# A rotary kernel whose swapped halves are copied out of PSUM by ScalarE instead of moved by DMA

## The reference

```python
def rope(x, positions):
    half = x.shape[-1] // 2
    ...
    x1, x2 = xf[..., :half], xf[..., half:]
    out = jnp.concatenate([x1 * cos - x2 * sin, x2 * cos + x1 * sin], axis=-1)

qa = rope(...); ka = rope(...)          # 24 heads each
qd = rope(...); kd = rope(...)          # 8 x 2 halves each
```

## Time and profile before

| | |
|---|---|
| median of 3 runs | 877.96 us (875.67 to 879.02) |
| the profiled execution, own time | 879.07 us |
| its span, first to last instruction | 877.3 us |
| TensorE busy | 818.3 us, 93% |
| VectorE, ScalarE, GpSimd busy | 471.5, 359.8, 482.6 us (54, 41, 55%) |
| mean granted TensorE clock | 0.982 of full |

### The profile page before, as it was taken

One profiled execution on the slowest core, in us unless ns is written; L12 is line 12 of the kernel. 1 busy time (PEld: TensorE's weight loads), 2 busy tenths in 40 slices (PEclk: granted clock), 3 DMA queues, 4 the chain that ended last, 5 costly groups with the idle time before them and its releaser, 6 DMA issues.

```text
span 877.3 us, 12629 instructions
## 1 busy us (share of the span) xinstructions
PE 818.3 (93%) x4622; PEld 687.9 (78%) x4622; DVE 471.5 (54%) x751; ACT 359.8 (41%) x774; POOL 482.6 (55%) x625
## 2 busy tenths in 40 slices
PE   1579799999999999999998999999899999999997
PEld 0468589788888888888877878778777777888897
DVE  2785678454454536323568669759756644102622
ACT  3334444344444344432444454454546542223410
POOL 2564655345655647245858359759645637736300
PEclk9979899999999999999998999999999999999999
DMA  9774284222333233324353133333121213333521
GB/s 251 198 217 105 67 285 121 86 73 86 96 121 94 80 117 97 97 72 137 105 138 96 49 110 97 109 97 86 57 88 49 60 37 117 99 97 106 182 97 49
DMA packets 92852, 94.87 MB, mean 108 GB/s; under 512 B 8269, under 2 KB 84086, under 8 KB 92662
## 3 DMA queue, kind: packets, MB, share of 16 engines
q1 hardware_dynamic: 92496, 93.64, 35.4%
q0 software_dynamic: 240, 0.39, 0.5%
q10 hardware_dynamic: 54, 0.02, 0.0%
HBM read 78.21 MB, written 5.34 MB: 95 GB/s over the span
## 4 chain that ended last, share of the span: by engine, by line
PE 69%; DVE 13%; issue 6%; DMA 4%; ACT 4%; SPq 2%; POOL 2%; DVEq 0%; POOLq 0%; ACTq 0%
PE proj L1502 50%; PE score L1381 4%; PE proj L1580 4%; PE sums L1427 3%; PE turned L1398 3%; DMA ada<-in_w_ada 2%; DVE dstat L1145 2%; PE score L1356 2%; ACT probs L891 2%; PE sums L1429 2%; DVE ada_sum L1025 1%; DVE dstat L1161 1%; DVE q_lo L1106 1%; DVE at_lo L1168 1%; ACT junk L923 1%
## 5 line engine op out<-in xcount | busy, mean ns | idle before, releaser
L694 POOL TENSOR_TENSOR w_lo<-raw,w_hi 128x256 fp32r<-128x256 f32 x392 | 316.4, 838 | 224.4 <-ACT w_hi L807 224.4
L1502 PE MATMUL proj<-h_hi,w_hi 128*128 128x512 f32 x608 | 253.3, 417 | 6.8 <-POOL h_lo L704 5.7
L1502 PE MATMUL proj<-h_hi,w_lo 128*128 128x512 f32 x608 | 241.8, 398 | 0.0
L1502 PE MATMUL proj<-h_lo,w_hi 128*128 128x512 f32 x608 | 241.0, 396 | 0.0
L1502 PEld LDWEIGHTS proj<-h_hi,w_hi 128*128 128x128 f32 x608 | 116.3, 191 | 42.1 <-issue 8.6
L1502 PEld LDWEIGHTS proj<-h_hi,w_lo 128*128 128x128 f32 x608 | 116.5, 192 | 26.6
L1502 PEld LDWEIGHTS proj<-h_lo,w_hi 128*128 128x128 f32 x608 | 116.7, 192 | 21.1
L807 ACT ACTIVATE w_hi<-raw 128x1024 fp32r<-128x1024 f32 x100 | 104.2, 1053 | 12.0 <-PE proj L1502 7.8
L719 POOL TENSOR_TENSOR rope_x<-rope_x,cos_t 128x512 f32<-128x512 f32 x36 | 55.9, 1552 | 69.5 <-DMA rope_s<-rope_x 69.5
L1168 DVE TENSOR_TENSOR at_lo<-turned,at_hi 128x512 fp32r<-128x512 f32 x64 | 43.9, 687 | 60.3 <-ACT at_hi L909 59.7
L891 ACT ACTIVATE probs<-score,dstat 128x512 f32<-128x512 f32 x64 | 43.4, 684 | 59.9 <-DVE dstat L1145 59.9
(11 more groups left out here) (245 smaller groups left out, 1522.1 us busy)
## 6 DMA issues: line engine op xcount, KB each, us to landing
raw<-in_w_in SPq DMA_DIRECT2D x88, 512.0 KB, 3.6
rope_s<-rope_x SPq DMA_DIRECT2D x144, 64.0 KB, 2.4
ada<-in_w_ada SPq DMA_DIRECT2D x16, 512.0 KB, 6.3
zd<-in_w_ada SPq DMA_DIRECT2D x8, 512.0 KB, 5.2
raw<-in_w_proj_b SPq DMA_DIRECT2D x8, 512.0 KB, 3.4
raw<-in_w_out SPq DMA_DIRECT2D x8, 512.0 KB, 4.1
rows_in<-window_rows SPq DMA_DIRECT2D x4, 792.0 KB, 4.9
window_rows<-rows_out SPq DMA_DIRECT2D x4, 528.0 KB, 4.9
```

Of the source, the lines that this page charges most:

```text
L694: ins = nc.gpsimd.tensor_tensor(lo[:, k, :], raw[:, n % RAW, k, :], hi.bitcast(F32)[:, k, :], ALU.subtract)
L1502: ins = mm(dst, left, right, start=k == 0 and n == 0, stop=k == nk - 1 and n == 2)
```

## The change

`rope_copy` gets four more ScalarE instructions. After the copy of the whole bank it copies the bank again, one quarter of the partitions at a time, each into the place of its neighbour in `rope_s` (or in the upper half of `zd`), with the same scale. The four DMAs of a tile, the four larger ones of the first four tiles, and their waits on SyncE go. GpSimd's cosine product now waits for the first copy only, VectorE's sine product for the last quarter, and TensorE's reuse of the bank for the last quarter too.

```diff
-        def swapped_wait(engine, tile):
-            n = rope_no[tile.u]
-            if n < 4:
-                engine.wait_ge(first_swapped, 64)
-            else:
-                engine.wait_ge(swapped[n % 4], 64 * (n // 4))
...
-            def swap_heads(tile):
-
-                n = rope_no[tile.u]
-                sp.wait_ge(rope_copied, n + 1)
-                if n >= 6:
-                    sp.wait_ge(rope_done, n - 1)
-                at, other = rope_place(tile)
-                for i in range(4):
-                    j = i ^ 1
-                    sp.dma_start(other[32 * i:32 * i + 32, :], at[32 * j:32 * j + 32, :]).then_inc(swapped[n % 4], 16)
...
-            sp.wait_ge(rope_copied, 4)
-            for i in range(4):
-                j = i ^ 1
-                sp.dma_start(zd[32 * i:32 * i + 32, 4:8, :], zd[32 * j:32 * j + 32, 0:4, :]).then_inc(first_swapped, 16)
...
-                for tile in tiles_done(t):
-                    if tile.kind in "qk":
-                        swap_heads(tile)
...
                 for tile in tiles[:4] if t == 8 else rope_at(t) if t >= 12 else []:
-                    swapped_wait(pool, tile)
+                    pool.wait_ge(rope_copied, rope_no[tile.u] + 1)
...
-                nc.scalar.activation(rope_place(tile)[0], proj[:, tile.u % 4, :], ACT.Copy,
-                                     scale=SCALE if tile.kind == "q" else 1.0).then_inc(rope_copied, 1)
+                at, other = rope_place(tile)
+                scale = SCALE if tile.kind == "q" else 1.0
+                bank = proj[:, tile.u % 4, :]
+                nc.scalar.activation(at, bank, ACT.Copy, scale=scale).then_inc(rope_copied, 1)
+                for i in range(4):
+                    j = i ^ 1
+                    ins = nc.scalar.activation(other[32 * i:32 * i + 32, :], bank[32 * j:32 * j + 32, :], ACT.Copy, scale=scale)
+                ins.then_inc(rope_swapped, 1)
...
             def rope_turn(tile):
                 n = rope_no[tile.u]
-                swapped_wait(dve, tile)
+                dve.wait_ge(rope_swapped, n + 1)
...
                 if old.kind in "qk":
-                    pe.wait_ge(rope_copied, rope_no[old.u] + 1)
+                    pe.wait_ge(rope_swapped, rope_no[old.u] + 1)
```

More of the change, by code:

```diff
@@ L375, in build @@
         gate_rows_loaded = sem("gate_rows_loaded")
-        first_swapped = sem("first_swapped")
-        swapped = [sem(f"swapped{i}") for i in range(4)]
+        rope_swapped = sem("rope_swapped")
         rows_stored = sem("rows_stored")
```

## The result

The changed kernel takes 925.88 us (median of 4 executions, 921.94 to 931.39) beside 878.49 us for the kernel before (4 executions, 875.67 to 879.15): a ratio of 1.057 with a 95% interval of 1.053 to 1.061 (the two medians alone give 1.054; the ratio is what the means give against the seven executions of the kernel before that stand beside the first experiments, median 876.44). I had said 893 with a range of 881 to 902. The direction was right and the size was not: 47 us were lost where I had counted 15.

A forecast was written before the change was run, and what follows sets the result against it. The prediction took TensorE, busy 93%, and where it stands still as the bound. Start 5.0 + window stages 4.2 + differential stages 8.2 - credit 2.0 = 15.4 us, giving 893 us, range 881 to 902.

The forecast's parts named there:

- The price of a quarter: Each ScalarE quarter copy was taken at 0.49 us, 1.96 us for each of 40 tiles.
- The start: Twenty ScalarE copies before the table load, instead of four, make TensorE's first scores later; 5.0 us lost.
- The window stages: The high part of the turned probabilities comes 1.96 us later, beyond TensorE's reserve in five ticks; 4.2 us lost.
- The reserve of 1.19 us: Stages 2 to 4: time from the low part's end at 232.07 to TensorE's read at 233.26.
- the two places of stage 1: Window stage 1: late maxima and exponentials exceed a reserve of 0.99 us before TensorE transposes; 1.9 us lost.
- The three reads of stages 2 to 4: Window stages: TensorE waits 0.77 us for the low part in each of three ticks; 2.3 us lost.
- The differential stages: Twelve rope copies under attention steps delay the high part beyond small reserves; 8.2 us lost.
- The credit: VectorE's sine products get shorter as earlier cosine products on GpSimd meet them less often; minus 2.0 us.
- No overlap, and the clock: Rival, chance 0.12: quarters cost 0.60 us each and two new stalls lower TensorE's clock; 904 us.
- Only the start: Rival, chance 0.18: late high parts in later stages are swallowed, only the start's 5 us is lost; 883 us.
- quarters at a quarter of the price: Rival, chance 0.07: a quarter copy costs 0.20 us, a tile 0.80 us more; 879 us.
- faster: Rival, chance 0.05: cosine products out of VectorE's way give back 6.7 us in the differential stages; 873 us.

The follow-up runs named there:

- the halved run: The changed kernel with each quarter copy made as two copies of 256 columns; 935.8 us in one execution.
- e5_three_parts: The changed kernel with three ScalarE copies in place of four quarters, the upper half's swap left out; 903.91 us, ratio 1.029.
- e8_one_whole: The changed kernel with one copy of all 128 partitions in place of the four quarters, the swap left out; 879.92 us, ratio 1.001.
- e2_rest_by_dma: The changed kernel with only the first four tiles swapped by ScalarE's quarters, the other 36 by DMAs as before; 890.21 us, ratio 1.014.

## Why the prediction was wrong

**The price of a quarter** ("I take 0.49"). Wrong by choice of row: I took the step between two whole copies, which begin in the same partitions, and had the no-overlap bound of 0.60 as well. It is 0.60 to 0.61, and 2.54 us for a tile with the two edges, not 1.96. The Trainium skill ("ScalarE: Activation LUTs", section "What ACT_TABLE_LOAD costs") lets neighbours overlap by 93 ns; in the halved run they do, by 90, but only within one quarter of the partitions.

**The start: 5.0, measured 8.6 in the trace and 8.8 by undoing it (6.7 to 12.0 in the traces with the same start).** The mechanism was right, down to the order (table load, weights, low part, cosine product, addition). The table load came 8.5 us later, not 7.1, although the first copy began 0.9 us earlier (75.84); the first addition was at 95.54, not 94.3, 7.3 us late against 6.1. The remaining 1.3 us came behind it. At my own price, in `e5_three_parts`, the start is 7.9 us late, of which 1.8 lie ahead of the first copy. The 1.1 us that I took off for loads without a swap ahead of them and a clock that comes back sooner was not there. With a wait of 7.6 us at 98.7 and one of 3.0 at 109.7 in place of one of 5.0, TensorE had the lower clock for longer around the start: over 30 to 175 us it costs 10.3 us before, and over 30 to 180 us 13.7 in the changed kernel. "TensorE's first scores near 108.5" were at 109.7.

**The window stages: 4.2, measured 11.4.** The reserve of 1.19 us was right: 2.54 - 1.19 = 1.35 against a wait of 1.26, and at a delay of 1.96 a wait of 0.68 in each of the three places against 0.77. At my own price the transpositions lose 3.7 us there. Waits at the true price are 6.4, and the clock, which I left at nothing, adds 3.4.

That 3.7 is near 4.2 is in part luck, since the two places of stage 1, 1.9 us of the sum, cost far less, and the one whose rows are shown was misread. These are the transposition of the earlier trace rows and the exponentials of the earlier trace rows in the changed kernel:

```profile
179.55 0.62 PE L1378 MATMUL turned<-ident,probs 128*128 128x128 f32 x4
...
180.09 0.47 ACT L879 ACTIVATE probs<-score,rows_out 128x256 f32<-128x256 f32 x1 [1.36 <-DVE rows_out L1132]
```

The transposition starts ahead of these exponentials, so it does not need them, and it is as late as the start made it and no more. The reserve of 0.99 us was none; the one that counts is that of the next transposition, which is hardly later either (8.58 against 8.55 us). From 171 to 230 us of before the transpositions lose 0.9 us in the changed kernel and 0.3 at my own price. The three reads of stages 2 to 4 make up for it: 2.8 us at my own price, not 2.3.

**The differential stages: 8.2, measured 23.0.** Here too the waits at my own price were right: 8.8 us in `e5_three_parts`. At the true price they are 12.3. The clock adds 10.3 (6.9 at my own price). My fear that "delays overlap and do not add" was unfounded.

**The credit: minus 2.0, measured zero or the other way.** VectorE's sine product of the steady part takes 1.01 us in the mean, not 0.98, and its median went from 0.69 to 0.93 us. The earlier cosine products did meet it less often, 6 of 36 times where it was 17. But that was not what made it long. By the timelines of before it takes 0.69 us at 11 of the 12 places where only a cosine product runs beside it. Of the long ones, 1.2 us and more, 14 of 16 before and 15 of 18 after stand beside GpSimd's low part of the weights, which the change left as it was. `e8_one_whole`, free of the DMAs and with a fifth of the quarters' delay, is not faster than before.

**The rivals.** "No overlap, and the clock" had both failing parts and still stopped at 904. Its 7.3 us for the price were near (between the run with three parts and the changed kernel the waits grow by 4.3 us in the window stages and 3.5 in the differential ones); its clock was not. It took the 1.8 us of one stretch for two places, where the changed kernel has two stretches in the window stages and three more than before in the differential ones, three of its six there twice as long. "Only the start" fell by the 35.7 us that `e2_rest_by_dma` gives back; "quarters at a quarter of the price" and "faster" fell with the 589 ns.

The step that failed most is thus that a new wait of TensorE was priced at its length alone. Of the 32 us that the sum lacked, some 14 are clock, 6 are waits of both stages at the true price of a quarter (18.7 against 12.4), 3.6 the start, 2 the credit, and 4 the distance of the changed kernel's median from its profiled execution; the last 2 I can't assign.

## What to carry to other kernels

An instruction's place in its engine's order costs, not its engine's total: here the same 160 copies cost 47 us ahead of the instruction for which TensorE waits and 4 us behind it. Before work is moved to a half-idle engine, look for the next instruction in its order whose consumer has a reserve, and put the work behind it. And where TensorE is near full, price a new wait at its length plus a stretch at the lower clock that may follow it: behind two of three waits of 1.3 us it did, and doubled their cost.

## What the runs showed of the hardware

ScalarE copies of 32 partitions take as long as whole ones (589 against 597 ns at 512 columns, 367 at 256), and one that begins in another quarter of the partitions does not start before the one ahead ends (0.37 against 0.28 us from start to start). The first of three waits of 1.26 us was followed, 2.7 us after its end, by some 3.5 us at 1.2 GHz, the second by a like stretch, the third by none; waits of 0.68 us at the same three places were followed by none. With seven short matmuls in the wait and 0.55 us idle behind them the clock fell at two of the three places, and with five wide ones at none. Of VectorE's sine products (128x512), those of 1.2 us and more stand beside GpSimd's low part of the weights at 29 of 34 places, in the two kernels together; of the 38 of 0.69 us two do.
